# A two-block transformer kernel: the first four weight splits of the second half move behind the last pick

## The reference, cut to what matters

```python
def peer(h, w_q, sub_keys, u_tab, v_tab):        # per chunk of 128 tokens
    ...
    s_top, i_top = lax.top_k(s, PEER_TOPK)        # 8 heads x 2 x 16 keys
    ...
    best, pos = lax.top_k(cand.reshape(...), PEER_TOPK)
    g = jax.nn.softmax(best, axis=-1)
    ue = jnp.take(u_tab, idx, axis=0)             # 128 experts per token
    ve = jnp.take(v_tab, idx, axis=0)
    act = jax.nn.gelu(jnp.einsum('thkd,td->thk', ue, t, ...), approximate=False)
    return jnp.einsum('thk,thkd->td', (g * act).astype(t.dtype), ve)
...
x = x + g2 * peer(h2, ...)                        # first block ends: rmsnorm(x, final_g)
for i in range(2):                                # second block
    y = mlstm_mixer(x, ...) if i % 2 == 0 else pool_mixer(x, ...)
    x = layer_norm(ALPHA * x + y, ...)
    x = layer_norm(ALPHA * x + memory_cross_attn(x, mem_k, mem_v, ...), ...)
    x = layer_norm(ALPHA * x + sq_relu_mlp(x, ...), ...)
```

## Time and profile before

| what | value |
|---|---|
| median of 3 runs | 3041.62 us (3040.8 to 3056.24) |
| the profiled execution | 3060.01 us, its span 3058.2 us |
| TensorE busy | 2754.8 us, 90% of the span |
| VectorE, ScalarE, GpSimd busy | 2102.1, 1249.0, 615.7 us |
| granted TensorE clock, mean | 0.957 of full speed |
| moved by DMA | 830.23 MB, mean 271 GB/s |

### The profile page before, as it was taken

How to read it: one execution, slowest core, us unless ns; L and a number is a source line. 1 busy time by engine, 2 the same in 40 slices (tenths; PEclk the granted TensorE clock), 3 DMA queues, 4 the chain that set the end, 5 groups by cost and what they waited for, 6 DMA issues and landing times. The chain is left out here.

```text
span 3058.2 us, 41815 instructions
## 1 busy us (share of the span) xinstructions
PE 2754.8 (90%) x14628; PEld 2083.7 (68%) x14628; DVE 2102.1 (69%) x4574; ACT 1249.0 (41%) x2944; POOL 615.7 (20%) x531
## 2 busy tenths in 40 slices
PE   6999998989888888688898999687999999999998
PEld 6777788444444444355576777355888889998998
DVE  6895556888878887656685666854546576675887
ACT  3333325444434443555453222452533443433544
POOL 0000001444444444432232333220000000010000
PEclk9999999999999999899997999798999999999999
DMA  6541234999999999999898999885433445543554
GB/s 237 181 170 49 60 87 155 421 420 420 420 418 420 419 414 417 374 419 400 346 413 332 410 417 417 349 331 195 140 130 98 137 142 189 180 156 106 145 185 139
DMA packets 157705, 830.23 MB, mean 271 GB/s; under 512 B 16704, under 2 KB 22080, under 8 KB 91840
## 3 DMA queue, kind: packets, MB, share of 16 engines
q0 software_dynamic: 73728, 536.90, 42.8%
q1 hardware_dynamic: 78240, 271.85, 25.9%
q10 hardware_dynamic: 5536, 18.88, 1.7%
HBM read 825.47 MB, written 2.10 MB: 271 GB/s over the span
## 5 line engine op out<-in xcount | busy, mean ns | idle before, releaser
L750 POOL DMA_INDIRECT slots<-in_experts,consts x306 | 363.5, 1188 | 1104.1 <-DVE consts L2436 524.5
L2461 DVE SCALAR_TENSOR_TENSOR slots<-slots,work 128x1024 f32<-128x1024 f32 x306 | 374.8, 1225 | 106.5 <-DMA slots<-in_experts,consts 95.1
L2060 DVE TENSOR_TENSOR wlo<-w,whi 128x1024 fp32r<-128x1024 f32 x259 | 314.7, 1220 | 71.0 <-ACT whi L1498 70.1
L1078 PE MATMUL psum<-slots,acc 128*128 128x512 f32 x636 | 308.2, 627 | 51.9 <-ACT acc L1716 44.6
L1498 ACT ACTIVATE whi<-w 128x1024 fp32r<-128x1024 f32 x259 | 272.4, 1053 | 149.9 <-PE psum L798 139.0
L1078 PEld LDWEIGHTS psum<-slots,acc 128*128 128x128 f32 x636 | 121.3, 197 | 213.2 <-issue 129.3
L783 PE MATMUL psum<-xres,w 128*128 128x256 f32 x1040 | 240.0, 387 | 0.0
L750 POOL DMA_INDIRECT split_slots<-in_experts,consts x149 | 181.7, 1219 | 281.0 <-issue 105.2
L783 PEld LDWEIGHTS psum<-xres,w 128*128 128x128 f32 x1040 | 198.0, 193 | 47.8 <-issue 21.5
L1704 ACT ACTIVATE consts<-consts 128x1 f32<-128x1 f32 x512 | 100.4, 196 | 315.1 <-DVE slots L2461 181.6
L2461 DVE SCALAR_TENSOR_TENSOR split_slots<-split_slots,work 128x1024 f32<-128x1024 f32 x149 | 182.5, 1225 | 36.2 <-DMA split_slots<-in_experts,consts 30.0
(11 more groups left out here) (370 smaller groups left out, 6047.5 us busy)
## 6 DMA issues: line engine op xcount, KB each, us to landing
w<-in_stream SPq DMA_DIRECT2D x424, 512.0 KB
back_w<-in_back SPq DMA_DIRECT2D x64, 512.0 KB, 3.7
arena<-in_wmod SPq DMA_DIRECT2D x4, 2048.0 KB, 17.1
arena<-in_wmod ACTq DMA_DIRECT2D x8, 1024.0 KB, 6.5
acc<-in_wmod ACTq DMA_DIRECT2D x8, 1024.0 KB, 6.9
slots<-in_experts,consts POOLq DMA_INDIRECT x306
split_slots<-in_experts,consts POOLq DMA_INDIRECT x149
xres<-in_xT SPq DMA_DIRECT2D x1, 2048.0 KB, 9.6
```

What stands on the lines that cost most here:

```text
L750: pool.indirect_dma_start(out=slots[slot], out_offset=None, in_=a["experts"], in_offset=bass.IndirectOffsetOnAxis(ap=indices[:, p:p + 1], ...
L1078: mm = pe.matmul(bank(6 + half), diag(p), v[:, half * T:(half + 1) * T], start=(c == 0), stop=(c == PICKS - 1))
L2060: dve.tensor_tensor(wlo[:, s, :, :].rearrange("p k n -> p (k n)"), w32[:, s, :], whi[:, s, :, :].rearrange("p k n -> p (k n)").bitcast(F32 ...
L2461: dve.scalar_tensor_tensor(u, u, 1.0, tokens[:, p // PICKS, :], ALU.mult, ALU.mult, accum_out=inner[:, c:c + 1]).then_inc(sem("dotted"), 1)
```

## The change

The four split slots stay in the gather's ring to the last pick, so `SPLIT_PICKS` goes: the distance from a gather to the pick before in its slot stays 13 up to pick 492 and is 11 from 493 on. The splits of tiles 229 to 232 leave their places in `xo1` and stand in the norm of `lstm1`: on ScalarE behind its 8 squares, on VectorE behind the 8 sums of squares and ahead of the statistics. The ring's last pick, 511, now has slot 15 instead of slot 2.

```diff
-FIRST_PICKS, SPLIT_PICKS, BACK_PICKS = 96, 474, 490
+FIRST_PICKS, BACK_PICKS = 96, 490
...
-        if p == SPLIT_PICKS:
-            for slot in (12, 13, 14, 15):
-                free.remove(slot)
...
                 if n >= NTILES or direct(n):
                     return
+                if n in range(DIRECT.stop, DIRECT.stop + RING):
+                    return
+                upper(n, turn)
+
+            def upper(n, turn=0):
+
                 s = n % RING
-                if n == DIRECT.stop:
-                    act.wait_ge(sem("pick_used"), ON_PE[SPLIT_PICKS])
-                    act.wait_ge(sem("pick_added"), ON_DVE[SPLIT_PICKS])
                 act.wait_ge(w_loaded[s], turn * 64 + 16 * (n // RING + 1))
...
                 squares(ni, lambda k: xres[:, k, cols], H, ready=ready, w=wh)
+                if half:
+                    act.wait_ge(sem("pick_used"), ON_PE[NPICKS])
+                    act.wait_ge(sem("pick_added"), ON_DVE[NPICKS])
+                    for m in range(RING):
+                        upper(DIRECT.stop + m)
                 weigh_picks(n - 1, True)
                 root(ni, H)
...
                 if n >= NTILES or direct(n):
                     return
+                if n in range(DIRECT.stop, DIRECT.stop + RING):
+                    return
+                lower(n, turn)
+
+            def lower(n, turn=0):
+
                 s = n % RING
                 dve.wait_ge(sem("w_upper"), turn * 16 + split_count(n))
...
                     add_square(ni, k, H, wh)
+                if half:
+                    for m in range(RING):
+                        lower(DIRECT.stop + m)
                 statistics(ni, EPS, H)
```

## The result

Over 20 runs of each, the changed kernel takes 3042.06 us (3029.4 to 3050.18) and the kernel before 3056.62 us (3040.8 to 3073.45): the ratio is 0.9945, with a 95% interval of 0.9931 to 0.9959, or 16.8 us less (12.5 to 21.1); the two medians differ by 14.6 us. The profiled execution of after took 3043.07 us, its span 3041.2 us, against 3060.01 and 3058.2.

What follows compares the result with a forecast made beforehand. The prediction took TensorE, busy for 90% of the span, as the bound, so only its idle or slow time could be gained. 6.3 + 10.0 - 0.7 + 0.6 = 16.2 us off the median 3041.62 gave 3025.4 us, range 3015 to 3037.

Steps and rivals of the forecast that it cites:

- The ring: Before picks 486 and 487: gather 487 goes out earlier, TensorE's idle time falls; gain 6.3 us, lower end 2.5.
- The 1.4 us for the clock: Part of the ring's gain: the pair of picks 486 and 487 takes 1.95 us instead of 3.34 after the shorter stop.
- the unnamed 2.43 us: Wait before VectorE's reduction of the attention's scores, no engine named; assumed hidden, otherwise the ring gains only 2.5 us.
- The splits leave `xo1`: In `xo1`, TensorE's stops before picks 506 and 507 and before 510 and 511 go; gain 10.0 us, lower end 8.3.
- The turn: Copies and turn behind the last pair: 0 to 1.4 us lost, 0.7 taken; all fast would gain up to 4.
- The norm of `xo1`: Without VectorE's fourth split, TensorE's spread is last before the first scaling; gain 0.6 us.
- The norm of `lstm1`: The moved splits hide behind TensorE's two back tiles with 0.6 us of cover left; cost 0, uncovered 5.3 us.
- SP's queue: Loads of tiles 233 and 234 go out later, waiting for splits, but land before ScalarE asks for 233; cost 0.
- (1): Rival: the ring adds little, transfers are late or the unnamed wait follows the scores; gain 10 to 12 us; 20%.
- (2): Rival: the splits are exposed in the norm of `lstm1`, back tiles early or weights late; gain 11 us; 10%.
- (4): Rival: slower, gathers keep transfers full and weight tiles reach TensorE late in `xq1` and `xo1`; up to 3059 us; 4%.
- Rival (3): The turn behind the last pair runs fast; gain 20 to 21 us, 3021 us; 10%.

Runs made afterwards that it cites:

- experiment 2: The kernel before with the split slots leaving the gather ring at pick 490 instead of 474, splits still in `xo1`: 3052.95 us, ratio 0.9989.
- experiment 1: The changed kernel with splits in the norm of `lstm1`, but the split slots leaving the ring at pick 474 as before: 3051.59 us, ratio 0.9982.
- experiment 3: The changed kernel, but ScalarE still waits in `xo1` for tiles 229 to 232 to land, without splitting there: 3050.66 us, ratio 0.9979.
- experiment 4: The changed kernel, but in `xo1` ScalarE waits for each of tiles 229 to 232 and copies it onto itself: one run, 3049.27 us.
- after again: The changed kernel measured and profiled once more, nothing changed, as a control: 3044.11 us, ratio 0.9959 to the kernel before.
- experiment 5: The changed kernel with each of the four splits in the norm done twice on ScalarE and VectorE: 3050.6 us, ratio 0.9979.
- before again: The kernel before, nothing changed, run once more for a second profile: one run, 3056.68 us.
- experiment 7: The changed kernel with ScalarE making the weights of picks 486 and 487 ahead of the attention's exponentials, likewise in `xq0`: 3038.61 us, ratio 0.9954.
- experiment 9: The changed kernel with weights ahead of the exponentials and five unread products on TensorE before the turns of chunks 2 and 3: 3027.77 us, ratio 0.9897.

## Why the prediction was right and wrong

**The ring: right in its chain, a little high.** The idle time fell from 7.04 to 2.09 us, as worked out (2.0 left), and experiment 2 gives 2.09 by itself. Two terms inside were not. The 1.4 us for the clock were not had: pair and tile 216 took 7.17 us (2013.17 to 2020.34) after the short stop as well, against 6.92 before (2016.93 to 2023.85), since the clock fell inside the pair. And the unnamed 2.43 us were no fixed part of before; in its second profile they are absent. The ring is worth 5.0 us of idle time against the first profile of before, 3.3 against experiment 1 and 2.4 against the second profile of before, where the range given was 2.5 to 6.3. The gather side was right but for a slip, pick 487 had the slot of pick 478 and not 477, which changes nothing in the sum: gather 487, in a split slot now, went out 18.7 us earlier than the earlier trace rows have it, 20 with the 1.3 us by which after was behind:

```profile
1981.19 1.96 POOL L747 DMA_INDIRECT split_slots<-in_experts,consts  x1 [4.88 <-PE psum L1090]
```

**The splits leave `xo1`: right.** Forecast 10.0, measured 10.2 (last pair less the pair behind tile 216: 2102.43 - 2020.34 = 82.09 for 92.25), and 9.0 in the segment of experiment 1. What the prediction did not see is why the stop was so long: I read the 8.2 us as the price of a load with gathers in flight, and experiments 3 and 4 show that about 4 of them hang on the short ring. The two parts overlap there: by the profiles of experiments 3 and 4, with the long ring and the splits left in `xo1`, some 4 of the 10 us would already have come.

**The turn: the mechanism was listed, the size was a coin.** I took -0.7, capped a fast turn at 4, and gave it 10%. The cap was too low by its own rows: eight of the turn's 32 rows ran fast before, not four, and the other 24 at their spacing of 0.43 us in place of 0.22 are 4.9 us. The profiled execution had a fast turn, and with the sums behind it, at full clock too, it was worth 5.6 (2120.34 to 2134.26 is 13.92; 2106.68 to 2114.96 is 8.28). But after again had a slow one. Over the ten profiles whose chunk 3 had no fill, the turn took 7.33 us in four and 11.4 to 13.9 in six. The reasoning from one execution each ("both turns speak against it") had no ground. The rest of the term's miss is that the square sums and statistics behind the turn share its clock.

**The norm of `xo1`:** from the statistics' sums to the first scaling 3.18 us became 2.16, a gain of 1.0 for 0.6. **The norm of `lstm1`:** forecast 0, measured 0.5, because TensorE's back tiles took 9.88 for 9.34 us; the splits ended 1.39 us ahead of the statistics (0.6 forecast), and experiment 5 shows what it costs if they end later. **SP's queue: right.** Tiles 233 and 234 went out late, and still ScalarE did not wait for 233:

```profile
2130.22 1.46 SPq L676 DMA_DIRECT2D w<-in_stream  x2
```
```profile
2145.88 1.05 ACT L1498 ACTIVATE whi<-w 128x1024 fp32r<-128x1024 f32 x1
```

**The sum and the time.** The saving was right: 16.2 us forecast, a ratio of 0.9947 to the median of 3041.62; measured 0.9945, with 12.5 to 21.1 us as its interval. That it came so close is in part luck. In the profiled pair the ring gave 1.2 us less than forecast and the turn 6.3 more, and 2.9 were given back where I had written that nothing gives the time back; and the ring's 5.1 us held some 2 us that belong to one execution, and the turn's 5.6 us come from a fast turn, seen in 4 executions of 10.

The predicted time was not right: 3025.4 us, range 3015 to 3037, against 3042.06. The step that failed is "I take the same amount off the median of 3041.62". That median came from three runs of 3040.8, 3041.62 and 3056.24, with a profiled execution at 3060.01 that stood apart from them; over 20 runs it is 3056.62, 15 us higher. The same 16.2 us taken off the 3060.01 are 3043.8, and after's profiled execution took 3043.07. I noted that one run showed 15 us of play and then let the range go up by only 12. A range built from the same terms around a level between 3041 and 3060 would have held the result. Of the rivals, (1), (2) and (4) as causes of a smaller gain are out or small: the ring's stop went as forecast, the splits were not exposed, no tile came late; only of the unnamed wait in (1) does something remain, since it was missing in the second profile of before and the ring's gain was 2.4 us against that one. Rival (3), the fast turn, is true of some executions whatever the change: experiments 1, 2 and 5 and after had it, before, before again, after again and experiments 3, 4 and 7 did not.

**What stays open.** The parts' times do not add cleanly: experiments 1 and 2 gain 5.5 and 3.4 us by their ratios, each with an interval of some 5 us to either side, and after 16.8 and, taken again, 12.5; from the profiles they overlap only where experiment 3 shows it. The times of experiments 1, 3 and 5 lie higher than their profiled stops would have them (gains of 5.5, 6.4 and 6.4 us, each with about 6 us to either side); after was not run again beside them, so whether this is play or a cost that the profiles don't show is open. So the split of the gain into parts rests on single profiled executions, and only the whole gain on the times. What the 2.43 us wait was is not known. Nor did any run show what made chunk 3's turn fast in four executions and slow in six. The Trainium skill (TensorE: Matmul & The Clock Gate, What's actually happening) says that the number of products that a kernel runs at the lower clock at its start differs from run to run. The traces agree in the middle of a kernel too, with 7.33 and 11.95 us for the same instructions.

## What to carry to other kernels

When several stops of one engine sit 15 to 90 us apart, cost each from its own chain, and then ask whether they share a resource: here the short ring delayed the gathers, these delayed a weight tile, and this held up ScalarE, its picks and TensorE. Work moved behind an engine's last job is free only up to the cover that the slowest engine leaves, which can be read off as one wait (1.39 us here); beyond that it is paid in full (4.6 us for 4.6 over the cover). Do not hang an absolute time on three runs when the profiled one stands 18 us from their median; forecast a ratio, and let the range hold the level's play.

## What the runs showed of the hardware that I had not expected

- A stretch of small products (64 columns each) behind 2.30 us of idle time ran at 2.4 GHz throughout in 4 of 10 executions (7.33 us, granted clock 1.00) and mostly or wholly at 1.2 GHz in the others (11.4 to 13.9 us, 0.58 in before, 0.50 in experiment 3); chunk 2's took 11.9 to 13.7 us in 12 of 12. With the idle time filled with 2.43 us of products that nobody reads, it was fast in 4 of 4 (three of chunk 3, one of chunk 2). For chunk 3 alone three fast ones would come by chance in 6 cases of 100 (0.4 to the third power). With needless work at both turns the kernel took 3027.77 us, against 3038.61 without it (experiments 9 and 7).
- The play of this kernel from run to run goes with the clock granted to TensorE, its mean over an execution. The 20 runs of after go from 3029.4 us at a mean of 0.963 to 3050.18 at 0.956, with a correlation of -0.92: the same instructions, 20 us apart.
- A 512 KB load that took 8.2 us beside gathers that filled the DMA engines (420 GB/s) took about 4 us at 105 to 113 GB/s (before and experiment 3).
